# Attention scores of two heads issued in turn from two halves of the partitions, with masks and maxima regrouped, in a transformer block on one core

## The chip, the cores and the metric

The kernel runs on one core of one Trainium2 chip, in one launch. The metric is the device time of that launch in microseconds; lower is better. The core has five engines with a queue each: TensorE (PE, matmuls; PEld is its weight load), VectorE (DVE), ScalarE (ACT), GpSimd (POOL) and SyncE (SP, which here issues nearly all DMAs). They run side by side and wait for one another by semaphores.

## The reference, cut to what matters

One layer of a hybrid block on 512 tokens of width 1024: adaptive norm, a wide input projection, a gated linear attention (GLA) branch, a dilated attention branch, a merge, and a convolutional feed-forward part. The change is in the dilated attention. It has 3 groups of 4 heads of width 64; group 0 has dilation 1, group 1 dilation 4, group 2 dilation 16 (within 512 tokens the last two are both computed as 4 residues of 128 tokens, the last with a mask that keeps every fourth distance).

```python
q = rotary(aq...); k = rotary(ak...)
for g, (window, dilation) in enumerate(ATTN_GROUPS):       # per group, per head
    s = einsum('brhnid,brhnjd->brhnij', qb, kc) * (Dh ** -0.5)   # Dh = 64
    s = where(valid, s, -inf)
    m = max(s, axis=-1); p = exp(s - m); denom = sum(p)
    o = einsum('brhnij,brhnjd->brhnid', p, vc) / denom
    lse = m + log(denom)
o = sum(softmax(lse over groups) * o_g)
```

Everything is float32. The big projections are computed as three products of a high and a low part of each operand; the attention scores are plain float32 matmuls with a contraction of 64.

## The kernel before, in words

**Order of the work.** Each engine has one program, written out by hand. A list of weight units (256 columns of a weight matrix each) sets the order: value weights, six `qk` units (pair p of heads, group g), the low-rank unit `lr`, then per GLA head h the units `gqk`, `gv`, `gr`, and so on. For a unit ACT writes the high part (`split_hi`, L673), DVE the low part (`split_lo`, L1228), and TensorE multiplies in `product`, two tiles of 24 x 128x512 matmuls (L1773 to L1775, `three`). A tile takes one of two accumulator banks, so tile i+2 waits until the evacuation of tile i has freed its bank. The pieces of other work are put between the tiles: `attention(p, i)`, i from 0 to 6, exists on PE, DVE and ACT. For pair p=0 its parts stand between the tiles of the `qk` units of pair 1, `lr` and `gqk`; for p=1 between those of GLA head 0 and the first of head 1.

**A pair of heads.** The weights of unit (p, g) give q and k of both heads of the pair. DVE rotates them (`rotate`, L1298, L1299, L1302) into `rope`, SP copies them with eight DMAs (`shuffle`, L501) to `qk`, where a head's 64 dimensions stand on partitions 0 to 63, and the two heads beside each other along the free dimension. Parts 0 and 1 of `attention` on PE are `scores(hh)` for heads hh = 2p and 2p+1. A head has four score banks: bk 0 and 1 of group 0 (3 blocks of 256 columns and one of 128), bk 2 of group 1 and bk 3 of group 2 (4 blocks of 128 each). One fp32 matmul of the program is two weight loads and two matmuls in the trace. For p=0, part 0 does the first three banks of head 0, and part 1 the rest of head 0 and all of head 1. The banks are `side[bk]`, one for each bk, and the second head of a pair waits for the masks of the first.

**Masks and maxima.** On DVE `mask_and_max(hh)` adds a mask while it moves a bank to `S` in SBUF (L1323) and then takes row maxima (L1331 to L1337, L1342). When both heads are done, SP writes the maxima to DRAM and reads them back in the other order of tokens (`exchange(p)`, L533 and L538), DVE makes `negm` (part 3: L1355, L1359), ACT takes the exponentials (`exps`, parts 3 and 4, L798), PE transposes `S` (parts 4 and 5, L1928) and multiplies with the values (parts 5 and 6, L1947 to L1955). On SP's queue `shuffle(3)` stands ahead of `exchange(0)`; it overwrites `qk` and therefore waits until all scores of pair 0 are done (`sc_done` 8). ACT's evacuation of the tiles of `gqk` of head 0 (L928) waits for all scores of pair 1, since `q_in` lies where `qk` lay.

In DVE's order, after unit `qk` (1,1) has been split, part 1 stands ahead of the rotation of that unit's first tile.

Of the kernel before, what the change touches and what calls it, by code (L numbers as in the profile page):

```python
# [7 lines left out]
F32 = mybir.dt.float32  # L8
# [4 lines left out]
ALU = mybir.AluOpType  # L13
# [3 lines left out]
P = 128  # L17
SEQ = 512
D = 1024
KT = D // P  # L20
NB = SEQ // P
# [6 lines left out]
DH = 64  # L28
# [143 lines left out]
def hybrid_block_kernel(nc, x, c, positions, ada_w, ada_b, norm1_w, w_in, gate_w2, gate_b, gla_norm_w,  # L172
# [3 lines left out]
    with ctx:  # L176
# [29 lines left out]
        def region(*places):  # L206
# [26 lines left out]
        qk, rope, oa_hi, oa_lo, ocomb, osum, orec, oa32, rope_t, v_ext, S, PT, mx, mx_other, mg, negm = region(  # L233
            ("qk", 0, [DH, GROUPS, 2, 2, SEQ], F32), ("rope", 24, [P, 2, 2, SEQ], F32),
            ("oa_hi", 32, [P, 2, SEQ], F32R), ("oa_lo", 36, [P, 2, SEQ], F32R),
# [3 lines left out]
            ("PT", 95, [P, 1920], F32), ("mx", 102.5, [P, 8, 2], F32), ("mx_other", 102.625, [P, 8, 2], F32),  # L239
            ("mg", 102.75, [P, 2, 4], F32), ("negm", 107, [P, 8, 2], F32))  # L240

# [169 lines left out]
        BANK_W = [512, 384, 512, 512]  # L411

        def score_blocks(bk):

            if bk == 0:
                return [(0, 2 * P, 1), (2 * P, 2 * P, 2)]
            if bk == 1:
                return [(0, 2 * P, 3), (2 * P, P, 0)]
            return [(r * P, P, NB + r) for r in range(DIL)]
# [11 lines left out]
        def _(sp):  # L431
# [61 lines left out]
            def shuffle(j):  # L493

                p, g = divmod(j, GROUPS)
                sp.wait_ge(rope_sum, j + 1)
                if j == GROUPS:
                    sp.wait_ge(sc_done, 8)
                for half in range(2):
                    for a in range(4):  # L500
                        sp.dma_start(qk[32 * half:32 * half + 32, g, a // 2, a % 2, :],  # L501
                                     rope[32 * a:32 * a + 32, j % 2, half, :]).then_inc(qk_in[j % 2], 16)
# [633 lines left out]
        def _(dve):  # L1136
# [166 lines left out]

            def mask_and_max(hh, banks=range(4)):

                p, hd = divmod(hh, 2)
# [4 lines left out]
                for bk in banks:  # L1311
                    dve.wait_ge(sc_done, 4 * hh + bk + 1)
                    if hh >= 2:
                        dve.wait_ge(tr_ps, 4 * (hh - 2) + bk + 1)
                    at, w = BANK_AT[bk], BANK_W[bk]
                    dst, src = S[:, hd, at:at + w], side[bk][:, 0:w]
# [7 lines left out]
                for bk in banks:  # L1324
                    dve.wait_ge(msk_done, 4 * hh + bk + 1)
                    at = BANK_AT[bk]
                    if hd == 0 and bk == 0 and p > 0:
# [5 lines left out]
                    elif bk == 1:  # L1333
                        dve.tensor_reduce(mx[:, 3:4, hd], S[:, hd, at:at + 2 * P], AX.X, ALU.max)
                        dve.tensor_reduce(mx[:, 0:1, hd], S[:, hd, at + 2 * P:at + 3 * P], AX.X, ALU.max)
                    else:
                        dve.tensor_reduce(mg[:, bk - 2, :], S[:, hd, at:at + 4 * P].rearrange("p (a n) -> p a n", a=DIL),  # L1337
                                          AX.X, ALU.max).then_inc(mx1_done, 1)
                if 3 not in banks:
                    return  # L1340
                dve.wait_ge(mx1_done, 2 * hh + 2)
                dve.tensor_tensor(mx[:, NB:2 * NB, hd], mg[:, 0, :], mg[:, 1, :], ALU.max).then_inc(mx_done, 1)  # L1342
                dve.wait_ge(mx_done, hh + 1)

            def attention(p, i):

                if (p, i) == (0, 0):
                    mask_and_max(0, range(3))
                elif i in (0, 1):
                    if (p, i) == (0, 1):  # L1350
                        mask_and_max(0, range(3, 4))
                    mask_and_max(2 * p + i)
                if i == 3:
# [201 lines left out]
            for p in range(2):  # L1555
                for g in range(GROUPS):
# [8 lines left out]
                    elif g == 1:  # L1565
                        split_lo(n + 1)
                        attention(0, 1)
                        rotate(GROUPS + g, 0)
                        attention(0, 2)
# [197 lines left out]
        def _(pe):  # L1767
# [125 lines left out]

            def scores(hh, banks=range(4)):
                p, hd = divmod(hh, 2)
                if hh == 0:
                    pe.wait_ge(vw_act, NB)
                    pe.wait_ge(vw_dve, NB)
                for bk in banks:
                    if hh >= 1:  # L1900
                        pe.wait_ge(msk_done, 4 * (hh - 1) + bk + 1)
                    if hd == 0:
                        j = GROUPS * p + max(bk - 1, 0)
                        pe.wait_ge(qk_in[j % 2], 16 * 8 * (j // 2 + 1))
                    if hd == 0 and p > 0:
                        pe.wait_ge(pt_act if bk < 2 else pt_dve, 4 * p)
                    if bk < 2:
                        blocks = [(0, 1), (2 * P, 2)] if bk == 0 else [(0, 3), (2 * P, 0)]
                        for col, b in blocks:
                            lo = max(b - 1, 0) * P  # L1910
                            keys = slice(lo, (b + 1) * P)
                            last = pe.matmul(side[bk][:, col:col + (b + 1) * P - lo], qk[:, 0, 0, hd, b * P:(b + 1) * P],  # L1912
                                             qk[:, 0, 1, hd, keys], start=True, stop=True, skip_group_check=True)
                    else:
                        for r in range(DIL):
                            tok = slice(r * P, (r + 1) * P)
                            last = pe.matmul(side[bk][:, r * P:(r + 1) * P], qk[:, bk - 1, 0, hd, tok],  # L1917
                                             qk[:, bk - 1, 1, hd, tok], start=True, stop=True, skip_group_check=True)
                    last.then_inc(sc_done, 1)

# [38 lines left out]
            def attention(p, i):  # L1959

                if (p, i) == (0, 0):
                    scores(0, range(3))
                elif (p, i) == (0, 1):
                    scores(0, range(3, 4))
                    scores(1)
                elif i in (0, 1):
                    scores(2 * p + i)
                if i == 4:
# [400 lines left out]
```

## Time and profile before

| | us |
|---|---|
| median of 3 runs | 918.63 (918.57 to 919.01) |
| the profiled execution, its own time | 917.4 |
| its span in the trace | 915.6 |
| TensorE busy | 898.0 (98%) |
| VectorE busy | 494.4 (54%) |
| ScalarE busy | 368.7 (40%) |

The profiled execution is one run, 1.2 us below the median of the others. Its time is 1.8 us longer than the span of instructions in the trace. Busy time of TensorE includes overlap of matmuls in the pipeline, so the mean duration of a matmul is longer than the distance from one to the next. The granted TensorE clock was 0.997 over the whole execution.

### The profile page before, as it was taken

The numbers are of one execution on the slowest core, as the hardware profiler recorded it, in microseconds if no ns is written. First come the engines' busy times: TensorE is split into PE (matmuls) and PEld (weight loads), VectorE is DVE, ScalarE is ACT, GpSimd is POOL, SyncE is SP. The second block draws the span as 40 slices with busy tenths as digits, with TensorE's granted clock in tenths as the row PEclk, the third lists the DMA queues.
The fourth block names the chain that finished last, engine by engine and source line by source line (L and its number), as shares of the span: only waits on it lengthen the run. The fifth ranks groups of instructions, "written<-read, shape, count | busy, mean of one in ns | idle before, by whom it ended". The sixth has DMA issues, their size and how long they took to land.

```text
span 915.6 us, 11818 instructions
## 1 busy us (share of the span) xinstructions
PE 898.0 (98%) x4635; PEld 767.8 (84%) x4635; DVE 494.4 (54%) x580; ACT 368.7 (40%) x461; POOL 35.9 (4%) x33
## 2 busy tenths in 40 slices
PE   6999999999999999999999999999999999999996
PEld 6998888889898988888888888888888888888885
DVE  6878875636462646542544476555555556422223
ACT  6541226593534365332223345333333334322235
POOL 0010000000000000000021210000000000000003
PEclk9999999999999999999999999999999999999998
DMA  9976745115251525452233431333333332332202
GB/s 326 301 240 165 191 98 157 48 47 184 92 185 47 184 93 184 144 179 92 80 119 133 129 93 47 92 94 105 107 106 92 92 92 92 121 109 92 92 0 92
DMA packets 117133, 112.91 MB, mean 123 GB/s; under 512 B 7412, under 2 KB 107126, under 8 KB 114663
## 3 DMA queue, kind: packets, MB, share of 16 engines
q1 hardware_dynamic: 116375, 110.21, 38.6%
q10 hardware_dynamic: 720, 2.16, 0.7%
q8 instruction: 27, 0.44, 0.2%
q14 instruction: 11, 0.09, 0.0%
HBM read 104.80 MB, written 4.21 MB: 119 GB/s over the span
## 4 chain that ended last, share of the span: by engine, by line
PE 92%; DVE 3%; SPq 2%; DMA 1%; issue 1%; ACT 0%; DVEq 0%; ACTq 0%
PE bank L1773 27%; PE bank L1774 26%; PE bank L1775 26%; DVE ada_in L1155 1%; PE bank L2280 1%; DMA ada_in<-in_ada_w_dram 1%; SPq L446 1%; PE bank L1917 1%; PE bank L1955 1%; PE bank L2045 1%; PE bank L2013 1%; PE bank L1912 1%; PE bank L1928 1%; PE bank L1889 1%; SPq L510 1%
## 5 line engine op out<-in xcount | busy, mean ns | idle before, releaser
L1773 PE MATMUL bank<-h_hi,w_hi 128*128 128x512 f32 x672 | 264.7, 394 | 0.0
L1775 PE MATMUL bank<-h_hi,w_lo 128*128 128x512 f32 x672 | 261.7, 389 | 0.0
L1774 PE MATMUL bank<-h_lo,w_hi 128*128 128x512 f32 x672 | 261.6, 389 | 0.0
L1775 PEld LDWEIGHTS bank<-h_hi,w_lo 128*128 128x128 f32 x672 | 126.1, 188 | 26.6
L1773 PEld LDWEIGHTS bank<-h_hi,w_hi 128*128 128x128 f32 x672 | 126.2, 188 | 25.9 <-issue 0.2
L1774 PEld LDWEIGHTS bank<-h_lo,w_hi 128*128 128x128 f32 x672 | 126.2, 188 | 25.4 <-issue 0.2
L1228 DVE TENSOR_TENSOR w_lo<-raw,w_hi 128x2048 fp32r<-128x2048 f32 (+2 forms) x44 | 81.0, 1854 | 86.9 <-ACT w_hi L673 86.9
L1235 DVE TENSOR_TENSOR w_lo<-raw,w_hi 128x2048 fp32r<-128x2048 f32 x31 | 71.1, 2293 | 86.3 <-ACT w_hi L681 86.3
L1727 DVE SCALAR_TENSOR_TENSOR conv<-bank,vecs,conv 128x511 f32<-128x511 f32 x88 | 65.7, 748 | 65.8 <-ACT conv L1087 60.3
L681 ACT ACTIVATE w_hi<-raw 128x2048 fp32r<-128x2048 f32 x31 | 59.1, 1906 | 69.3 <-PE bank L1775 69.3
L673 ACT ACTIVATE w_hi<-raw 128x2048 fp32r<-128x2048 f32 (+2 forms) x42 | 67.9, 1630 | 46.9 <-DMA raw<-in_w_in_dram 34.2
L1087 ACT ACTIVATE conv<-bank,vecs 128x512 f32<-128x512 f32 x44 | 34.2, 779 | 104.7 <-PE bank L1775 104.7
L1773 PE MATMUL bank<-hs_hi,w_hi 128*128 128x512 f32 x176 | 68.6, 389 | 0.0
L1775 PE MATMUL bank<-hs_hi,w_lo 128*128 128x512 f32 x176 | 68.5, 389 | 0.0
L1774 PE MATMUL bank<-hs_lo,w_hi 128*128 128x512 f32 x176 | 68.5, 389 | 0.0
L1775 PEld LDWEIGHTS bank<-hs_hi,w_lo 128*128 128x128 f32 x176 | 33.0, 188 | 6.9
L1774 PEld LDWEIGHTS bank<-hs_lo,w_hi 128*128 128x128 f32 x176 | 33.0, 188 | 6.8
L1773 PEld LDWEIGHTS bank<-hs_hi,w_hi 128*128 128x128 f32 x176 | 33.0, 188 | 6.8
L1773 PE MATMUL bank<-w_hi,h_hi 128*128 128x256 f32 x128 | 36.5, 285 | 0.1
L1775 PE MATMUL bank<-w_hi,h_lo 128*128 128x256 f32 x128 | 36.2, 283 | 0.0
L1774 PE MATMUL bank<-w_lo,h_hi 128*128 128x256 f32 x128 | 36.2, 283 | 0.0
L1262 DVE SCALAR_TENSOR_TENSOR ada_acc<-raw,c_silu,ada_acc 128x2048 f32<-128x2048 f32 x14 | 32.9, 2346 | 0.0
(282 smaller groups left out, 1253.7 us busy)
## 6 DMA issues: line engine op xcount, KB each, us to landing
raw<-in_w_up_dram SPq DMA_DIRECT2D x44, 512.0 KB, 5.0
raw<-in_w_in_dram SPq DMA_DIRECT2D x17, 1024.0 KB, 5.3
raw<-in_ada_w_dram SPq DMA_DIRECT2D x16, 1024.0 KB, 5.5
raw<-in_w_in_dram SPq DMA_DIRECT2D x22, 512.0 KB, 5.3
raw<-in_w_down_dram SPq DMA_DIRECT2D x22, 512.0 KB, 3.7
ada_in<-in_ada_w_dram SPq DMA_DIRECT2D x16, 512.0 KB, 9.5
raw<-in_w_gla_branch_dram SPq DMA_DIRECT2D x4, 1024.0 KB, 4.9
raw<-in_w_out_dram SPq DMA_DIRECT2D x4, 1024.0 KB, 5.0
```

What stands on the lines that cost most here:

```text
L446: sp.dma_start(ada_first(j, half)[:, :, s_, :], ada_t[:, rows, s_, 2 * j * P:2 * (j + 1) * P]).then_inc(ada_landed[2 * j + half], 16)
L510: sp.dma_start(dst[:, rows, :], w_in_v[:, rows, at:at + width]).then_inc(first_in[n] if part == 0 else landed[n], 16)
L673: last = act.activation(hv, r, ACT.Copy)
L681: act.activation(w_hi[:, slot, :], raw[:, slot, :], ACT.Copy).then_inc(hi_done, 1)
L1087: act.activation(conv[:, s, t, :], bank[2 * (1 - s) + t][:, :], ACT.Identity, scale=vecs[:, bass.ds(i + (V_CW2 + t * FT), 1)], bias=vecs[: ...
L1228: last = dve.tensor_tensor(lv, r, hv.bitcast(F32), ALU.subtract)
L1235: dve.tensor_tensor(w_lo[:, slot, :], raw[:, slot, :], w_hi[:, slot, :].bitcast(F32), ALU.subtract).then_inc(raw_used, 1)
L1262: ins = dve.scalar_tensor_tensor(ada_acc[:, :], src, c_silu[:, k:k + 1], ada_acc[:, :], ALU.mult, ALU.add)
L1727: ins = dve.scalar_tensor_tensor(conv[:, s, t, tap:SEQ], src[:, 0:SEQ - tap], vecs[:, bass.ds(i + (col + t * FT), 1)], conv[:, s, t, tap:S ...
L1773: pe.matmul(out_ap, wh, xh, start=first, stop=False, skip_group_check=True)
L1774: pe.matmul(out_ap, wh, xl, start=False, stop=False, skip_group_check=True)
L1775: return pe.matmul(out_ap, wl, xh, start=False, stop=last, skip_group_check=True)
```

## The change

It has four parts.

1. `qk` becomes `[P, GROUPS, 2, SEQ]`: head 0 of the pair on partitions 0 to 63, head 1 on partitions 64 to 127. The eight DMAs of `shuffle` keep their number and size and change their targets.
2. `scores(p, bk)` issues each block for head 0 and then the same block for head 1, from the two halves of the partitions. The banks are `side[bk % 2 * 2 + hd]`. Part 0 does bk 0 and 1 of both heads, part 1 bk 2 and 3 of both. bk 2 and 3 wait for the masks of bk 0 and 1; for p=1 all four banks wait for the copies of pair 0 at the start.
3. On DVE `mask_and_max` becomes `masks(p, bk)` and `maxima(p, bk)`, each for both heads. A part does its four masks ahead of its four (or six) maxima. The two last combinations stand together at the end of part 1.
4. In the unit (1,1), DVE rotates the unit's first tile ahead of part 1 of pair 0.

```diff
-            ("qk", 0, [DH, GROUPS, 2, 2, SEQ], F32), ("rope", 24, [P, 2, 2, SEQ], F32),
+            ("qk", 0, [P, GROUPS, 2, SEQ], F32), ("rope", 24, [P, 2, 2, SEQ], F32),
...
-            ("mg", 102.75, [P, 2, 4], F32), ("negm", 107, [P, 8, 2], F32))
+            ("mg", 102.75, [P, 2, 2, 4], F32), ("negm", 107, [P, 8, 2], F32))
...
+        def score_bank(bk, hd):
+            return side[bk % 2 * 2 + hd]
...
-                        sp.dma_start(qk[32 * half:32 * half + 32, g, a // 2, a % 2, :],
+                        at = a % 2 * DH + 32 * half
+                        sp.dma_start(qk[at:at + 32, g, a // 2, :],
                                      rope[32 * a:32 * a + 32, j % 2, half, :]).then_inc(qk_in[j % 2], 16)
...
+            def masks(p, bk):
...
+                for hd in range(2):
+                    dve.wait_ge(sc_done, 8 * p + 2 * bk + hd + 1)
+                    if p > 0:
+                        dve.wait_ge(tr_ps, 8 * (p - 1) + 4 * hd + bk + 1)
+                    dst, src = S[:, hd, at:at + w], score_bank(bk, hd)[:, 0:w]
...
             def attention(p, i):
-                if (p, i) == (0, 0):
-                    mask_and_max(0, range(3))
-                elif i in (0, 1):
-                    if (p, i) == (0, 1):
-                        mask_and_max(0, range(3, 4))
-                    mask_and_max(2 * p + i)
+                if i in (0, 1):
+                    for bk in (2 * i, 2 * i + 1):
+                        masks(p, bk)
+                    for bk in (2 * i, 2 * i + 1):
+                        maxima(p, bk)
...
                     elif g == 1:
                         split_lo(n + 1)
+                        rotate(GROUPS + g, 0)
                         attention(0, 1)
-                        rotate(GROUPS + g, 0)
                         attention(0, 2)
                         rotate(GROUPS + g, 1)
...
+            def scores(p, bk):
+                if p == 0 and bk == 0:
+                    pe.wait_ge(vw_act, NB)
+                    pe.wait_ge(vw_dve, NB)
+                if p > 0 and bk == 0:
+                    pe.wait_ge(pt_act, 4 * p)
+                    pe.wait_ge(pt_dve, 4 * p)
+                if bk >= 2:
+                    pe.wait_ge(msk_done, 8 * p + 2 * (bk - 2) + 2)
...
+                for n, (col, queries, keys) in enumerate(parts):
+                    for hd in range(2):
+                        rows = slice(hd * DH, (hd + 1) * DH)
+                        last = pe.matmul(score_bank(bk, hd)[:, col:col + keys.stop - keys.start], qk[rows, g, 0, queries],
+                                         qk[rows, g, 1, keys], start=True, stop=True, skip_group_check=True)
+                        if n == len(parts) - 1:
+                            last.then_inc(sc_done, 1)
```

On TensorE, part 0 of pair 0 between two product tiles is, in the kernel before (L1773 to L1775 are the tiles, L1912 is group 0, L1917 groups 1 and 2; `x3` counts matmuls in a row, and both heads use partitions 0 to 63):

```order
L1775 MATMUL bank<-h_hi,w_lo 128x512
L1912 MATMUL bank<-qk 128x256 x3
L1912 MATMUL bank<-qk 128x128
L1917 MATMUL bank<-qk 128x128 x4
L1773 MATMUL bank<-h_hi,w_hi 128x512
```

and now (L1780 to L1782 are the tiles, L1923 all scores):

```order
L1782 MATMUL bank<-h_hi,w_lo 128x512
L1923 MATMUL bank<-qk 128x256 x6
L1923 MATMUL bank<-qk 128x128 x2
L1780 MATMUL bank<-h_hi,w_hi 128x512
L1781 MATMUL bank<-h_lo,w_hi 128x512
```

Part 0 keeps eight matmuls; they are now all of group 0, and neighbours belong to different heads. Part 1 of pair 0, one tile later on TensorE, was:

```order
L1775 MATMUL bank<-h_hi,w_lo 128x512
L1917 MATMUL bank<-qk 128x128 x4
L1912 MATMUL bank<-qk 128x256 x3
L1912 MATMUL bank<-qk 128x128
L1917 MATMUL bank<-qk 128x128 x8
L1773 MATMUL bank<-h_hi,w_hi 128x512
```

and is now:

```order
L1782 MATMUL bank<-h_hi,w_lo 128x512
L1923 MATMUL bank<-qk 128x128 x16
L1780 MATMUL bank<-h_hi,w_hi 128x512
L1781 MATMUL bank<-h_lo,w_hi 128x512
L1782 MATMUL bank<-h_hi,w_lo 128x512
```

It keeps sixteen matmuls too, now all of 128 columns and of groups 1 and 2.

On VectorE, from the split of unit (1,2) (the weights `w_lo`) to the end of part 1, the kernel before has:

```order
L1228 TENSOR_TENSOR w_lo<-raw,w_hi 128x8x128 x2
L1323 TENSOR_TENSOR S<-bank,cst 128x512
L1337 TENSOR_REDUCE mg<-S 128x4
L1342 TENSOR_TENSOR mx<-mg 128x4
L1323 TENSOR_TENSOR S<-bank,cst 128x512
L1323 TENSOR_TENSOR S<-bank,cst 128x384
L1323 TENSOR_TENSOR S<-bank,cst 128x512 x2
L1331 TENSOR_REDUCE mx<-S 128x2
L1334 TENSOR_REDUCE mx<-S 128x1
L1335 TENSOR_REDUCE mx<-S 128x1
L1337 TENSOR_REDUCE mg<-S 128x4 x2
L1342 TENSOR_TENSOR mx<-mg 128x4
```

and now:

```order
L1233 TENSOR_TENSOR w_lo<-raw,w_hi 128x8x128 x2
L1303 TENSOR_TENSOR rope<-bank,cs 128x512
L1304 SCALAR_TENSOR_TENSOR rope_t<-bank,cs 128x512
L1327 TENSOR_TENSOR S<-bank,cst 128x512 x4
L1344 TENSOR_REDUCE mg<-S 128x4 x4
L1350 TENSOR_TENSOR mx<-mg 128x4 x2
```

The rotation of one tile (`rope`, `rope_t`) has moved ahead of the masks, and the masks and maxima of group 0 of the second head have moved to part 0, ahead of this piece.

## Rows read from the trace of the kernel before

**Rows 1.** The page: busy time and share of TensorE; then the chain's shares.

```profile
PE 898.0 (98%) x4635; PEld 767.8 (84%) x4635; DVE 494.4 (54%) x580; ACT 368.7 (40%) x461; POOL 35.9 (4%) x33
...
PE 92%; DVE 3%; SPq 2%; DMA 1%; issue 1%; ACT 0%; DVEq 0%; ACTq 0%
```

**Rows 2.** Groups on TensorE by shape: rows*weight columns, moving shape, count | busy us, mean ns.

```profile
L1917 PE MATMUL bank<-qk 64*128 64x128 f32 x64 | 8.1, 274 | 0.0
L1889 PE MATMUL bank<-ones,ada_acc 128*128 128x1 f32 x64 | 7.7, 237 | 0.0
L1912 PE MATMUL bank<-qk 64*128 64x256 f32 x24 | 6.1, 389 | 0.0
L2017 PE MATMUL bank<-q,enb 128*32 128x32 f32 x32 | 1.8, 199 | 0.0
```

**Rows 3.** The chain in order of time, score stretches: start us, us, what.

```profile
106.39 1.71 PE bank L1912 x8
108.10 0.89 PE bank L1917 x8
...
114.65 1.08 PE bank L1917 x8
115.74 1.52 PE bank L1912 x8
117.26 1.79 PE bank L1917 x16
...
154.88 1.71 PE bank L1912 x8
156.59 1.79 PE bank L1917 x16
...
167.64 0.61 ACT q_in L928
```

**Rows 4.** Timeline of DVE, parts 0 and 1 of pair 0: start us, us.

```profile
109.51 1.75 DVE L1323 TENSOR_TENSOR S<-bank,cst 128x512 f32<-128x512 f32 x3
111.17 0.68 DVE L1331 TENSOR_REDUCE mx<-S 128x2 f32<-128x512 f32 x1
...
112.29 0.68 DVE L1337 TENSOR_REDUCE mg<-S 128x4 f32<-128x512 f32 x1
112.88 2.35 DVE L1228 TENSOR_TENSOR w_lo<-raw,w_hi 128x1024 fp32r<-128x1024 f32 x2
...
117.42 2.35 DVE L1323 TENSOR_TENSOR S<-bank,cst 128x512 f32<-128x512 f32 x4
...
120.80 1.27 DVE L1337 TENSOR_REDUCE mg<-S 128x4 f32<-128x512 f32 x2
...
122.30 1.05 DVE L1298 TENSOR_TENSOR rope<-bank,cs 128x512 f32<-128x512 f32 x1
```

**Rows 5.** Timeline of SP's DMA issues, the maxima of pair 0.

```profile
119.14 5.66 SPq L501 DMA_DIRECT2D qk<-rope  x8
124.84 1.15 SPq L533 DMA_DIRECT2D mx_dram<-mx  x2
129.34 0.91 SPq L538 DMA_DIRECT2D mx_other<-mx_dram  x2
```

**Rows 6.** Timeline of ACT: exponentials of the first head of pairs 0 and 1.

```profile
132.69 3.95 ACT L798 ACTIVATE S<-S,negm 128x256 f32<-128x256 f32 x12 [7.36 <-DVE negm L1359]
...
181.40 3.94 ACT L798 ACTIVATE S<-S,negm 128x256 f32<-128x256 f32 x12
```

**Rows 7.** The chain in order of time, at the transposes of pair 0.

```profile
135.64 1.71 PE bank L1928 x15
```

**Rows 8.** Timeline of DVE, pair 1: masks, last combination, the maxima's return.

```profile
160.34 2.35 DVE L1323 TENSOR_TENSOR S<-bank,cst 128x512 f32<-128x512 f32 x4
...
170.60 0.17 DVE L1342 TENSOR_TENSOR mx<-mg 128x4 f32<-128x4 f32 x1
...
177.36 0.17 DVE L1355 TENSOR_TENSOR mx_other<-mx_other,mx 128x16 f32<-128x16 f32 x1 [2.49 <-DMA mx_other<-mx_dram]
```

More of the change, by code:

```diff
@@ L1302, in rotate @@
                     dve.tensor_tensor(rope[:, j % 2, :, :], rope[:, j % 2, :, :], rope_t[:, :, :], ALU.add).then_inc(rope_sum, 1)
-            def mask_and_max(hh, banks=range(4)):
-                p, hd = divmod(hh, 2)
+            def masks(p, bk):
                 prev_own, own = cst[:, C_MSK:C_MSK + 2 * P], cst[:, C_MSK + P:C_MSK + 2 * P]
@@ L1310, in mask_and_max @@
                 two = prev_own.rearrange("p (a n) -> p a n", a=1).broadcast_to((P, 2, 2 * P))
[L1311 to L1316, printed above, removed]
+                at, w = BANK_AT[bk], BANK_W[bk]
+                for hd in range(2):
[3 more added lines that the diff above has]
+                    dst, src = S[:, hd, at:at + w], score_bank(bk, hd)[:, 0:w]
                     if bk == 1:
@@ L1323, in mask_and_max, with maxima @@
                     dve.tensor_tensor(dst, src, m, ALU.add).then_inc(msk_done, 1)
-                for bk in banks:
-                    dve.wait_ge(msk_done, 4 * hh + bk + 1)
-                    at = BANK_AT[bk]
+            def maxima(p, bk):
+                at = BANK_AT[bk]
+                for hd in range(2):
+                    dve.wait_ge(msk_done, 8 * p + 2 * bk + hd + 1)
                     if hd == 0 and bk == 0 and p > 0:
@@ L1336, in mask_and_max @@
                     else:
-                        dve.tensor_reduce(mg[:, bk - 2, :], S[:, hd, at:at + 4 * P].rearrange("p (a n) -> p a n", a=DIL),
+                        dve.tensor_reduce(mg[:, hd, bk - 2, :], S[:, hd, at:at + 4 * P].rearrange("p (a n) -> p a n", a=DIL),
                                           AX.X, ALU.max).then_inc(mx1_done, 1)
-                if 3 not in banks:
+                if bk < 3:
                     return
-                dve.wait_ge(mx1_done, 2 * hh + 2)
-                dve.tensor_tensor(mx[:, NB:2 * NB, hd], mg[:, 0, :], mg[:, 1, :], ALU.max).then_inc(mx_done, 1)
-                dve.wait_ge(mx_done, hh + 1)
+                dve.wait_ge(mx1_done, 4 * (p + 1))
+                for hd in range(2):
+                    dve.tensor_tensor(mx[:, NB:2 * NB, hd], mg[:, hd, 0, :], mg[:, hd, 1, :], ALU.max).then_inc(mx_done, 1)
+                dve.wait_ge(mx_done, 2 * p + 2)
             def attention(p, i):
-                if (p, i) == (0, 0):
-                    mask_and_max(0, range(3))
-                elif i in (0, 1):
-                    if (p, i) == (0, 1):
-                        mask_and_max(0, range(3, 4))
-                    mask_and_max(2 * p + i)
+                if i in (0, 1):
[3 more added lines that the diff above has]
+                        maxima(p, bk)
                 if i == 3:
@@ L1892, in ada_part @@
                         last.then_inc(acc_ready, 1)
-            def scores(hh, banks=range(4)):
-                p, hd = divmod(hh, 2)
-                if hh == 0:
+            def scores(p, bk):
+                if p == 0 and bk == 0:
                     pe.wait_ge(vw_act, NB)
                     pe.wait_ge(vw_dve, NB)
[L1899 to L1919, printed above, removed]
@@ new lines, in scores @@
+                if p > 0 and bk == 0:
[3 more added lines that the diff above has]
+                    pe.wait_ge(msk_done, 8 * p + 2 * (bk - 2) + 2)
+                j = GROUPS * p + max(bk - 1, 0)
+                pe.wait_ge(qk_in[j % 2], 16 * 8 * (j // 2 + 1))
+                g = max(bk - 1, 0)
+                if bk < 2:
+                    parts = []
+                    for col, b in ([(0, 1), (2 * P, 2)] if bk == 0 else [(0, 3), (2 * P, 0)]):
+                        parts.append((col, slice(b * P, (b + 1) * P), slice(max(b - 1, 0) * P, (b + 1) * P)))
+                else:
+                    parts = [(r * P, slice(r * P, (r + 1) * P), slice(r * P, (r + 1) * P)) for r in range(DIL)]
@@ new lines, in scores @@
+                for n, (col, queries, keys) in enumerate(parts):
+                    for hd in range(2):
+                        rows = slice(hd * DH, (hd + 1) * DH)
[3 more added lines that the diff above has]
+                            last.then_inc(sc_done, 1)
@@ L1959, in attention @@
             def attention(p, i):
[L1961 to L1967, printed above, removed]
+                if i in (0, 1):
+                    for bk in (2 * i, 2 * i + 1):
+                        scores(p, bk)
                 if i == 4:
```

## The prediction

> **What bounds the kernel now.** I read the page first. TensorE is busy for 98% of the span, and 92% of the chain that ended last is TensorE [rows 1]. So only what shortens or stalls TensorE's own queue counts; DVE, ACT and SP matter where TensorE would wait for them. Next I read the chain in order of time where the scores stand [rows 3]. The reader is to see that score matmuls lie on the chain without a gap. Part 0 of pair 0 takes 1.71 + 0.89 = 2.60 us and part 1 takes 1.08 + 1.52 + 1.79 = 4.39 us, together 6.99 us. For pair 1 a part is a whole head, 1.71 + 1.79 = 3.50 us, and the second head repeats it (two such stretches): 7.00 us. All scores are 14.0 us in 96 trace matmuls. Third, the groups by shape [rows 2], to see how fast such matmuls follow one another, and last the timelines of DVE, SP and ACT [rows 4 to 6, 8], to see what comes due once TensorE is earlier.
>
> **Part by part: the scores on TensorE.** Nothing is removed: 24 blocks of 256 columns and 72 of 128 in the trace before and after. What can change is the distance between them. In the last stretch of groups 1 and 2 sixteen matmuls of 128 columns take 1.79 us, 0.112 us each [rows 3], though one lasts 274 ns [rows 2]. In the stretch at 115.74 six of 256 and two of 128 columns take 1.52 us; with 0.112 for the small ones that leaves 0.216 us for a large one. All of them use partitions 0 to 63, half the rows of the array. After the change neighbours use different halves. The trace has no two matmuls on different halves in a row, so this price is bounded from both sides:
> - Best: the halves work side by side. A program matmul is two trace matmuls on one half, A1 A2 B1 B2. A2 must follow A1, B1 can run beside A2, B2 beside the next A1. Each step of 0.112 (or 0.216) us then carries two. Part 0 (12 x 0.216 + 4 x 0.112 = 3.04 us in series) takes half, 1.52, plus 0.1 for the step that is half empty; part 1 (32 x 0.112 = 3.58) takes 1.79 + 0.06. That is 3.5 us for a pair in place of 7.0, a gain of 3.5 us for each pair.
> - Middle: every matmul is stepped by its weight load. The nearest rows are matmuls with one moving column: 64 of them are busy 7.7 us, 0.12 us each, as long as with 128 columns, so there the load of 128 weight columns sets the step; with 32 weight columns it is 1.8 / 32 = 0.056 us [rows 2]. The last row also says that a load and a matmul can be issued in 0.056 us, so issue alone doesn't forbid the best case. If loads of both halves share one path, a pair takes 48 x 0.112 = 5.4 us, a gain of 1.6.
> - Worst: no overlap, and each change of half waits for the matmul before to leave the array, 274 - 112 = 0.16 us. With 48 changes over the kernel that is a loss of 7.7 us.
>
> I take the best end. The 64-row operands leave the other half idle, the two heads write different PSUM banks (`side[0]` and `side[1]`, then `side[2]` and `side[3]`), and neither the issue rate nor the data forbids it. The Trainium skill, "TensorEngine Tiling (Array Packing)", Key Properties, says that different tiles can load weights and multiply in parallel; no run here shows it yet, and by it the sum is that of the best end. The Trainium skill, "TensorE: Matmul & The Clock Gate", LDWEIGHTS, says that a weight load goes by its columns and not by its rows. The trace agrees (0.12 against 0.056 us for 128 and 32 columns), and if this held for the pair as a whole, the sum would be that of the middle.
>
> **Pair 0 gives part of it back.** The transposes of pair 0 start at 135.64 on the chain, and 11 x 0.112 us later, at 136.9, comes the fourth bank [rows 7]. The exponentials of that bank end at 132.69 + 3.95 = 136.64 [rows 6]. So they are only 0.2 us ahead, and they must become earlier too. Their chain after the change, in the best case:
> - Masks of part 0 start at 109.51 as now (DVE is behind a rotation). Four masks last 2.3 us [rows 4], two times the maxima of group 0 at 112.29 - 111.17 = 1.1 each make 2.2, so part 0 ends at 114.0, not 112.9. The split takes 2.3 (116.3), the rotation that has moved ahead 2 x 1.0 (118.3), four masks 2.4 (120.7), four maxima 4 x 0.6 = 2.4 and the combinations 0.3: the maxima are ready at 123.4. Now they are ready at 122.3, where the rotation starts.
> - On SP `shuffle(3)` starts when the scores end. It would start at 115.8 in place of 119.14 and be through in 5.7 us, at 121.5. The writes of the maxima then wait for DVE until 123.4, in place of 124.84: 1.4 us earlier. The reads come 4.5 us behind the writes [rows 5], at 127.9. For pair 1 the whole way from the last combination to the use of the returned maxima is 177.36 - 170.60 = 6.8 us [rows 8]; the same from 123.4 gives 130.2. `negm` follows at 130.6. DVE is free by then: the tile that it rotates ahead of it would be rotated by about 129.
> - So the exponentials start at 130.6 in place of 132.69, 2.1 us earlier, and with the 0.2 of slack TensorE can be 2.3 us earlier at the transposes, of 3.5.
>
> The gain of pair 0 is thus 2.2 us (rounded down), and a new wait of about 1.2 us stands in the transposes. Behind it on TensorE are `lr`, the values and all later tiles, and ACT's copies and exponentials shift with it, so that none of them is late again.
>
> **The moved rotation** costs nothing by itself, as the same two instructions of 1.05 us. It has a use: in the kernel before they end at 122.30 + 2.0 = 124.3 [rows 4], just as TensorE wants that accumulator: its tile starts behind the scores at 119.05 and takes 114.65 - 108.99 = 5.66 us, to 124.7 [rows 3]. With TensorE 3.3 us earlier they would be late by that much if they had stayed; moved, they end at 118.3 and the tile begins at about 121.
>
> **Pair 1.** TensorE arrives 2.2 us earlier and gains 3.5 in parts 0 and 1. The masks, at 160.34 in the trace, follow the same shift to 158.1 and take 2.3 us; bk 2 needs the second mask at 159.3 and TensorE comes there at about 160, bk 3 needs the fourth at 160.4 and TensorE comes at 160.9. No wait. The last combination, 170.60 now [rows 8], comes after 158.1 + 2.3 + 2.2 + 2.4 + 2.7 = 167.7, so 2.9 us earlier; with the same exchange `negm` is there 0.4 us behind 177.36 - 2.9, at 174.9. The exponentials stand at 181.40 [rows 6] behind other work of ACT and move by 5.7 to 175.7. Slack 0.8 us, no new wait. ACT's L928 waits for all scores of pair 1 and starts at 167.64 and TensorE goes on behind its 0.61 us [rows 3]; this wait of 0.6 us stays, since scores are still last before it.
>
> **The rest.** The DMAs of `shuffle` keep number and size; their landing hides behind a tile of 5.4 us. The waits of part 0 for group 1's `qk` go away and cost nothing before. The semaphore for the copies of pair 0 is long set. Loads of weights are issued when a slot is freed, so they shift with the work; I cost them at nothing, and if one were late it would show on ACT's splits.
>
> **Sum.** 2.2 + 3.5 = 5.7 us off the profiled execution: 917.4 - 5.7 = 911.7. The median of the runs stands 1.2 above it, so 912.9; I say 913.0.
>
> **Rivals.**
> 1. Weight loads set the step (the middle bound). For: one column costs as much as 128. Against: those rows are on the same rows of the array, where a load and its forerunner can't be apart. The gain is 2 x 1.6 = 3.2 us, all kept, since pair 0 needs less than 2.3: 915.4. If a load is only started once the matmul before it has begun, just the distance between halves shrinks for the large blocks, 24 / 2 x 0.104 = 1.3 us: 917.3. I price the case at 916.
> 2. The halves do not overlap, the change does not do what it says: TensorE takes 14.0 us as before. DVE's last maxima of pair 1 come about 1 us later, which the slack of ACT hides. 918.6, within 0.3.
> 3. The other side: each change between halves drains the array. Place: the 48 changes in four stretches. Price: 0.16 us each, 7.7 us, 926.3. It would be slower by the margin from 1.84 / 48 = 0.04 us for a change, without overlap. For: 274 against 112 ns show how much of a matmul's life is in flight. Against: nothing in the trace changes tiles, and the entry from full tiles to 64 rows costs about 0.1 us.
> 4. The best case, but pair 0 keeps nothing, for instance because the writes of the maxima take as long as they like: 918.6 - 3.5 = 915.1. It belongs to the range of the forecast.
>
> **Numbers.** Forecast (halves overlap, 912.2 to 915) 0.57; loads set the step 0.21; no overlap 0.12; drain 0.10. A measurement of this kernel can tell 0.2%, 1.84 us, from no change. Faster: 0.57 and three quarters of 0.21, 0.73 less a little for what I don't see, 0.71. Same: 0.18. Slower: 0.11. The range for 8 in 10 reaches from 911.9 (nothing lost in pair 0 up to 1 us) to 918.6, which takes in the loads and half of the no-overlap case. Its likeliest part is 912.2 to 915.0.
>
> **What would show it.** Right: in the chain the scores of a pair take about 3.5 us, in two stretches of 1.6 and 1.85; neighbours start much less than 0.1 us apart; the rotation is ahead of the masks; the exponentials of pair 0 start near 130.6, and TensorE waits about 1.2 us for them in the transposes; those of pair 1 aren't waited for. Wrong: distances of 0.112 us for 128 columns (loads), or 0.27 (drain); exponentials later than 132, or a transposes stretch with no wait although TensorE is 3 us ahead; a wait for DVE's mask at bk 2 or 3 of pair 1.

## The result and the profile after

| | before | after |
|---|---|---|
| median of 6 runs each | 918.42 us | 912.43 us (912.18 to 912.98) |
| ratio, 95% interval | | 0.9936 [0.9923, 0.9949] |
| profiled execution, its span | 917.4, 915.6 | 912.18, 910.4 |
| TensorE busy | 898.0 | 891.1 |

The change makes the kernel faster by 6.0 us at the median; the interval is 4.7 to 7.1 us. The two profiled executions differ by 5.2 us. A second set of runs of the changed kernel gave 0.9946 [0.9934, 0.9958]. The forecast was 913.0. Part of the spread lies outside the span of instructions: the median span is 910.65 us in both sets of the changed kernel, while the medians of the time are 912.43 and 913.22, since the time outside the span is 1.8 us in some runs and 2.5 to 2.8 in others. Where small differences matter below, spans are compared too.

First the page of the changed kernel, part 1, and by shape the groups of score matmuls (columns as in [rows 2]):

```profile
PE 891.1 (98%) x4635; PEld 760.7 (84%) x4635; DVE 493.5 (54%) x580; ACT 368.7 (40%) x461; POOL 35.9 (4%) x33
```

```profile
L1923 PE MATMUL bank<-qk 64*128 64x128 f32 x72 | 4.9, 277 | 0.0
L1923 PE MATMUL bank<-qk 64*128 64x256 f32 x24 | 3.1, 393 | 0.0
```

The 96 matmuls are the same as in [rows 2], and one still lasts 277 or 393 ns. But together they are busy for 4.9 + 3.1 = 8.0 us, where [rows 2] have 8.1 + 6.1 = 14.2 us for 88 of the 96. They last as long as before and follow one another twice as fast. The other 4539 matmuls are unchanged, and the busy time of TensorE falls by 6.9 us. The span falls by 5.2, less than that: something of the gain is given back.

The timeline of TensorE (start us, us, what, then what ended the idle time before it) shows where the difference stands:

```profile
106.58 1.79 PE L1923 MATMUL bank<-qk 64*128 64x256 f32 x16
...
108.30 0.50 PE L1780 MATMUL bank<-h_hi,w_hi 128*128 128x512 f32 x1
...
113.96 2.06 PE L1923 MATMUL bank<-qk 64*128 64x128 f32 x32
...
115.95 0.50 PE L1780 MATMUL bank<-h_hi,w_hi 128*128 128x512 f32 x1
...
132.41 0.93 PE L1935 MATMUL bank<-cst,S 128*128 128x128 f32 x7
133.58 0.66 PE L1935 MATMUL bank<-cst,S 128*128 128x128 f32 x4 [0.25 <-ACT S L803]
134.75 0.66 PE L1935 MATMUL bank<-cst,S 128*128 128x128 f32 x4 [0.51 <-ACT S L803]
...
152.84 1.79 PE L1923 MATMUL bank<-qk 64*128 64x256 f32 x16
...
160.23 2.06 PE L1923 MATMUL bank<-qk 64*128 64x128 f32 x32
162.21 0.73 PE L1989 MATMUL bank<-w2s,lrT 98*128 98x512 f32 x2
```

The scores of pair 0 take 1.72 us from their start to the next tile in part 0 and 1.99 us in part 1, 3.7 us in place of 6.99 [rows 3]. The transposes (L1935), one stretch without a gap in [rows 7], are now in three pieces and wait for ScalarE's exponentials before the third and the fourth bank. The scores of pair 1 take 1.72 + 2.04 us on the chain below, and their masks don't hold them up.

The trace also has the start of each single matmul. In part 1 of pair 0 the first two start at 113.961 and 113.968, 7 ns apart, and from the second pair on such a pair follows every 0.112 us. The last of each head in bank 2, known by the semaphore that it raises, are 6 ns apart (114.845 and 114.851). So the blocks A1 A2 of head 0 and B1 B2 of head 1 do not run as A1, A2 beside B1, B2 beside the next A1: B1 starts beside A1, ahead of A2. Only the way in and out of a stretch costs more than the usual step: 0.214 us from the first matmul to the next on its half, and 0.201 from the last to the tile, against 0.112. The kernel before has the same (0.213 into part 1, 0.202 out of part 0), so a stretch takes 0.19 us beyond its steps.

The chain of the changed kernel, in order of time, goes another way in pair 0 (start us, us, what):

```profile
120.62 2.38 DVE mg L1344 x4
...
123.30 0.37 SPq L538
...
123.71 4.16 DMA mx_dram<-mx
...
127.89 0.36 SPq L543
...
128.29 2.01 DMA mx_other<-mx_dram
...
130.75 3.96 ACT S L803 x12
...
134.75 0.66 PE bank L1935 x4
...
152.91 1.72 PE bank L1923 x16
...
160.30 2.04 PE bank L1923 x32
```

Before, the chain stayed on TensorE through this stretch. Now it runs through the last maxima on VectorE, the write of the maxima to DRAM, the read, and the exponentials, and comes back to TensorE at 134.75.

VectorE is the one that releases the write here, but only just. On SP's timeline the shuffle ends at 122.86, 0.4 us before the maxima are written out:

```profile
116.31 0.38 SPq L479 DMA_DIRECT2D raw<-in_w_in_dram  x1
116.74 0.58 SPq L480 DMA_DIRECT2D raw<-in_w_in_dram  x1
117.44 5.42 SPq L506 DMA_DIRECT2D qk<-rope  x8
```

The shuffle starts 1.5 us behind the end of the scores (115.95). Ahead of it on SP's queue stand two weight loads. They are issued 0.02 us after VectorE has ended a split (116.29), and that split starts 1.0 us later than in the kernel before, as part 0 now has two times the maxima of group 0. In the profiles of e2 and d1 below, SP writes the maxima directly behind the shuffle (123.67 and 124.72), though they are ready since 123.56 and 123.54.

The wait itself varies from one execution to the next. In the profile of the second set of the changed kernel TensorE waits once, and not twice:

```profile
132.87 1.53 PE L1935 MATMUL bank<-cst,S 128*128 128x128 f32 x11
134.91 0.66 PE L1935 MATMUL bank<-cst,S 128*128 128x128 f32 x4 [0.51 <-ACT S L803]
```

The account in profiled time: up to the end of the transposes the changed kernel is 137.35 - 135.40 = 1.95 us ahead, and since its scores happened to start 0.27 us later, pair 0 gave 2.2 us. From there to the end of the scores of pair 1 it takes 26.94 us (135.40 to 162.34) in place of 30.21 (137.35 to 167.56), 3.3 us less. Behind that the distance stays at 5.2 us to the end.

### The profile page after: what moved, and what is told of

Same layout as the page of the kernel before. It is cut to its first block, busy times and chain, and to the rows that moved or that the text cites. A ratio compares the mean times of both kernels' runs of the same rounds, so it can differ in the third digit from the quotient of the medians.

```text
span 910.4 us, 11817 instructions
## 1 busy us (share of the span) xinstructions
PE 891.1 (98%) x4635; PEld 760.7 (84%) x4635; DVE 493.5 (54%) x580; ACT 368.7 (40%) x461; POOL 35.9 (4%) x33
## 3 DMA queue, kind: packets, MB, share of 16 engines
q10 hardware_dynamic: 720, 2.16, 0.7%
## 4 chain that ended last, share of the span: by engine, by line
PE 87%; DVE 5%; DMA 3%; SPq 2%; issue 1%; ACT 1%; DVEq 0%; ACTq 0%
PE bank L1780 25%; PE bank L1782 25%; PE bank L1781 25%; DVE ada_in L1160 1%; PE bank L2283 1%; DMA ada_in<-in_ada_w_dram 1%; SPq L450 1%; PE bank L1962 1%; PE bank L2048 1%; PE bank L2016 1%; DMA raw<-in_w_in_dram 1%; PE bank L1896 1%; PE bank L1935 1%; SPq L515 1%; PE bank L1957 1%
## 5 line engine op out<-in xcount | busy, mean ns | idle before, releaser
L1780 PE MATMUL bank<-h_hi,w_hi 128*128 128x512 f32 x672 | 264.7, 394 | 0.0
L1782 PE MATMUL bank<-h_hi,w_lo 128*128 128x512 f32 x672 | 261.7, 389 | 0.0
L1782 PEld LDWEIGHTS bank<-h_hi,w_lo 128*128 128x128 f32 x672 | 126.1, 188 | 26.6
L1780 PEld LDWEIGHTS bank<-h_hi,w_hi 128*128 128x128 f32 x672 | 126.2, 188 | 25.8 <-issue 0.2
L1780 PE MATMUL bank<-hs_hi,w_hi 128*128 128x512 f32 x176 | 68.6, 389 | 0.0
L1782 PE MATMUL bank<-hs_hi,w_lo 128*128 128x512 f32 x176 | 68.5, 389 | 0.0
L1782 PEld LDWEIGHTS bank<-hs_hi,w_lo 128*128 128x128 f32 x176 | 33.0, 188 | 6.9
L1780 PEld LDWEIGHTS bank<-hs_hi,w_hi 128*128 128x128 f32 x176 | 33.0, 188 | 6.7
L1780 PE MATMUL bank<-w_hi,h_hi 128*128 128x256 f32 x128 | 36.5, 285 | 0.1
L1782 PE MATMUL bank<-w_hi,h_lo 128*128 128x256 f32 x128 | 36.2, 283 | 0.0
```

The source lines that it names most:

```text
L1780: pe.matmul(out_ap, wh, xh, start=first, stop=False, skip_group_check=True)
L1782: return pe.matmul(out_ap, wl, xh, start=False, stop=last, skip_group_check=True)
```

## The experiments

Times are medians, and ratios are to the kernel before on the same chip. The changed kernel is the base unless said otherwise.

**Both heads on one half (e1).** The operands lie as in the kernel before, and the targets of `shuffle` with them; everything else is as changed.

```diff
-            ("qk", 0, [P, GROUPS, 2, SEQ], F32)
+            ("qk", 0, [DH, GROUPS, 2, 2, SEQ], F32)
...
-                        last = pe.matmul(..., qk[rows, g, 0, queries], qk[rows, g, 1, keys], ...)
+                        last = pe.matmul(..., qk[:, g, 0, hd, queries], qk[:, g, 1, hd, keys], ...)
```

Expected: 

> The changed kernel with the scores' operands of both heads on partitions 0 to 63 again, in turn, with the new banks, masks, maxima and rotation. Theory (the halves of the array overlap): scores take 14.0 us on the chain again, 0.112 us for 128 columns, the wait in the transposes of pair 0 goes, and the time is 918.4, within 0.6. Rival (the gain comes from the regrouped masks and the moved rotation): 912.4 to 914.

Measured: 918.25 us, ratio 0.9995 [0.9985, 1.0004]. The timeline of TensorE, its scores:

```profile
106.56 3.30 PE L1921 MATMUL bank<-qk 64*128 64x256 f32 x16
...
115.45 3.83 PE L1921 MATMUL bank<-qk 64*128 64x128 f32 x32
```

The whole gain is gone, so it comes from the halves; the regrouping and the moved rotation give nothing by themselves. The banks are those of the changed kernel, so the banks are not what lets the matmuls overlap. One detail was wrong: a wait of 0.51 us in the transposes is still there. The exponentials start at 133.68, 1.0 us later than in [rows 6], behind a read of the maxima that took 2.79 us on the chain. The 0.2 us by which they are in time in the kernel before is less than what the exchange varies by.

**Head by head within a bank (e2).** The halves stay, the order changes.

```diff
-                for n, (col, queries, keys) in enumerate(parts):
-                    for hd in range(2):
+                for hd in range(2):
+                    for n, (col, queries, keys) in enumerate(parts):
```

Expected: 

> The changed kernel with the two halves kept, but within a bank all blocks of head 0 ahead of those of head 1. Theory (only neighbours on different halves overlap): overlap is left at the seams, 8 in a pair, about 0.11 us each, so scores take some 12 us and the time is 916.5 to 917.5. Rival (work is spread over the halves whatever its order, since later matmuls are pulled ahead): as the changed kernel, 912.4.

Measured: 914.34 us, ratio 0.9948 [0.9935, 0.9961]. Neither theory gave this number. The timeline of TensorE:

```profile
106.85 1.89 PE L1923 MATMUL bank<-qk 64*128 64x256 f32 x16
114.35 2.82 PE L1923 MATMUL bank<-qk 64*128 64x128 f32 x32
```

In part 0 four matmuls follow one another on a half, and it loses 0.1 us. In part 1 eight do, and it takes 2.82 us, between 2.06 (in turn) and 3.83 (one half). A strict order, in which only the last of a run shares its step with the first of the next, would make 13 steps in part 0, ten of 0.216 us and three of 0.112, 2.5 us, and 29 steps of 0.112, 3.2 us, in part 1, each without the 0.19 us in and out. So the two halves don't take their matmuls strictly in the order of the program.

The starts of the single matmuls show how they do it. In part 1 the eight of head 0 in bank 2 start from 114.354 to 115.237, and the first of head 1 at 114.908, 6 ns behind the fifth of head 0. Three of head 0 have still to start then. At the next two changes of half it is again the fifth (115.457 and 115.462, then 116.011 and 116.017). In part 0, with four in a run, head 1 starts 14 ns behind the first of head 0, again past three.

**Two blocks and two (e5).** To pin that down, runs of four on a half in both parts:

```diff
-                for n, (col, queries, keys) in enumerate(parts):
-                    for hd in range(2):
+                for n, hd, (col, queries, keys) in [(m + i, hd, parts[m + i]) for m in range(0, len(parts), 2)
+                                                    for hd in range(2) for i in range(2)]:
+                    for _ in range(1):
```

Expected: 

> The changed kernel with two blocks of head 0 and then two of head 1 in turn, so that four trace matmuls follow one another on a half. Theory from the run head by head, where only runs of eight lost time (matmuls on the other half start ahead of some four waiting ones): part 1 takes 2.0 us as with one and one, 912.4. Rival (strict order, one shared step for each run of four): 25 steps of 0.112 us, 2.8 us for part 1, 914.

Measured: 913.07 us, ratio 0.9939 [0.9926, 0.9952], beside 913.22 us, 0.9946, for the changed kernel on that chip. The timeline:

```profile
106.92 1.89 PE L1924 MATMUL bank<-qk 64*128 64x256 f32 x16
114.43 2.16 PE L1924 MATMUL bank<-qk 64*128 64x128 f32 x32
```

Part 1 takes 2.16 us, not 2.8. Runs of four trace matmuls cost 0.1 us for a stretch, runs of eight 0.76. The starts fit e2: in part 1 the first of head 1 starts 14 ns behind the first of head 0, with three of head 0 still to start. So in these two kernels a matmul goes past three waiting trace matmuls of the other half and not past four: in e2, when the fourth of head 0 starts at 114.791 with four behind it, nothing of head 1 starts. What sets this reach no run shows.

**Scores twice, in turn (d1) and on one half (d2, from the kernel before).**

```diff
+                parts = parts + parts
```

In the kernel before the lists of blocks and of residues are doubled in the same way. Each block is computed twice into the same place.

Expected for d1: 

> The changed kernel with every score block computed twice into the same place, in turn between the halves. Theory (halves overlap, a pair's scores cost 3.75 us): 7.5 us more, less the 1.2 us of waiting in the transposes of pair 0, so about 918.7. Rival (each matmul is stepped by its weight load, 0.112 us): 10.8 us more, 922 to 923.

Expected for d2: 

> The kernel before with every score block computed twice into the same place. Both theories: 14.0 us more, 932.4; this is the price of the scores on one half measured on the whole kernel. Less would mean that part of the scores was not on the path.

Measured: d1 918.06 us, ratio 0.9997 [0.9988, 1.0006], 5.6 us above the changed kernel; d2 931.09 us, ratio 1.0139 [1.0124, 1.0155], 12.8 us (11.4 to 14.2) above the kernel before. The timelines, first d1, then d2:

```profile
106.83 3.31 PE L1924 MATMUL bank<-qk 64*128 64x256 f32 x32
...
115.73 3.84 PE L1924 MATMUL bank<-qk 64*128 64x128 f32 x64
...
135.97 1.87 PE L1936 MATMUL bank<-cst,S 128*128 128x128 f32 x15
```

```profile
161.56 3.30 PE L1912 MATMUL bank<-qk 64*128 64x256 f32 x16
164.70 3.73 PE L1917 MATMUL bank<-qk 64*128 64x128 f32 x32
```

Twice the matmuls in turn cost what the single ones cost on one half. The second 32 of part 1 add 3.84 - 2.06 = 1.78 us, 0.056 us each: half of 0.112, with nothing lost. With 3.31 - 1.79 = 1.52 for part 0 that is 3.3 us more for a pair, 6.6 in all; the kernel loses only 5.6, because the transposes of pair 0 have no wait any more (x15 in one piece). This supports both terms, the price of a pair and the wait. d2 doubles the scores on one half: the fence shows one head of pair 1. The expected 14.0 us took the way in and out of each stretch twice; the added matmuls alone are 24 x 0.216 + 72 x 0.112 = 13.2 us, and the median spans differ by 929.3 - 916.3 = 13.0. If each matmul were stepped by its weight load, d1 had been 922 or more.

**The rotation back behind part 1 (e3, e3b).**

```diff
-                        rotate(GROUPS + g, 0)
                         attention(0, 1)
+                        rotate(GROUPS + g, 0)
```

Expected: 

> The changed kernel with the rotation behind the masks and maxima of part 1 again. The rotation would end at about 123.1, and TensorE wants the accumulator at 121.4: a wait of 1.7 us before the tile. Theory: the wait of 1.2 us in the transposes, behind it, shrinks by as much, and the time is 912.6 to 913.2. Rival (waits add up): 914.1.

Expected of the repeat: 

> The changed kernel with the rotation behind part 1 again, a second time and beside the changed kernel. Its first profile shows TensorE waiting 1.34 us for the rotation and no longer for the exponentials. Theory: 0.5 us above the changed kernel. Rival (the waits add up): 1.3 us or more above it.

Measured: 914.22 us (five runs, two near 913.0 and three near 914.3), ratio 0.9944 [0.9930, 0.9957]; in the repeat 912.95 us, 0.9948 [0.9935, 0.9961], where the changed kernel had 913.22 and 0.9946. The timeline of TensorE of the first:

```profile
123.48 0.50 PE L1780 MATMUL bank<-h_hi,w_hi 128*128 128x512 f32 x1 [1.34 <-DVE rope_t L1304]
...
134.54 1.86 PE L1935 MATMUL bank<-cst,S 128*128 128x128 f32 x15
```

The wait is where it was expected, 1.34 us for the rotation (1.7 expected), and the one in the transposes is gone. So most of one wait replaces the other, and they do not add up. By the time alone the first set would have looked like the rival. The median spans are 911.5 and 911.2 us, 0.85 and 0.55 above the 910.65 of the changed kernel. The profiles agree: from the start of the scores of pair 0 to the gate matmuls behind those of pair 1 (L1989) it takes 56.17 and 56.36 us, and 55.63 and 55.35 in the two profiles of the changed kernel. The move of the rotation is worth some 0.5 to 0.9 us here, less than its wait, as the exponentials hold TensorE anyway. In e3 the maxima are ready at 121.38, but SP writes them at 122.94, behind the shuffle: the earlier maxima don't bring the exchange forward by as much.

**The moved rotation alone, in the kernel before (e4).** The same two lines.

Expected: 

> The kernel before with the moved rotation alone. Theory: it frees an accumulator that TensorE does not wait for, so 918.4 within 0.4; the maxima come 2 us later, hidden since the exchange stands behind the shuffle. Rival (the moved rotation is part of the gain): under 917.5.

Measured: 918.99 us, ratio 1.0013 [0.9999, 1.0027]. No gain. In its profile SP issues the write of the maxima directly behind the shuffle (125.81), as in [rows 5], so the later maxima, ready at 124.63, don't hold anything. TensorE does wait in the transposes here, which in the profile of the kernel before it didn't:

```profile
138.17 0.66 PE L1928 MATMUL bank<-cst,S 128*128 128x128 f32 x4 [0.36 <-ACT S L798]
```

From write to read the exchange took 5.0 us and not 4.5; as in e1, being in time by 0.2 us is no more than chance. The scores started 1.0 us later than in the profile of the kernel before, which is a difference between two executions and not the change's.

**The exchange of group 0 early (f1).** The maxima of group 0 are ready at the end of part 0. They are written ahead of the shuffle and read back ahead of the wait for the others.

```diff
+                if part == 0:
+                    sp.wait_ge(mx0_done, 6)
+                    sp.dma_start(own[0], mx[:, 0:NB, :]).then_inc(mx_out, 16)
+                    return
+                if part == 1:
+                    sp.wait_ge(mx_out, 16)
+                    sp.dma_start(mx_other[:, NB:2 * NB, :], other[1]).then_inc(mx_in, 16)
+                    sp.wait_ge(mx_done, 2)
+                    sp.dma_start(own[1], mx[:, NB:2 * NB, :]).then_inc(mx_out, 16)
+                    sp.wait_ge(mx_out, 32)
+                    sp.dma_start(mx_other[:, 0:NB, :], other[0]).then_inc(mx_in, 16)
+                    return
```

Expected: 

> The changed kernel with the exchange of the maxima of pair 0 in two steps: the maxima of group 0 are written before the shuffle and read back before those of groups 1 and 2 are ready; these follow alone. Theory (the exponentials of pair 0 hold TensorE through the exchange): negm comes when DVE is free, at about 129.7 and not 130.5, the wait in the transposes goes, 1.0 us less, 911.4. Rival (the wait comes back elsewhere, or the remaining DMAs take as long as all four): 912.4.

Measured: 911.36 us, ratio 0.9925 [0.9911, 0.9939], 1.1 us below the changed kernel's median of 912.43. Its timeline of SP's issues, of DVE and of TensorE:

```profile
124.24 0.58 SPq L542 DMA_DIRECT2D mx_other<-mx_dram  x1
124.86 0.45 SPq L544 DMA_DIRECT2D mx_dram<-mx  x1
126.57 0.37 SPq L546 DMA_DIRECT2D mx_other<-mx_dram  x1
```

```profile
129.28 0.17 DVE L1376 TENSOR_TENSOR mx_other<-mx_other,mx 128x16 f32<-128x16 f32 x1
```

```profile
132.49 1.86 PE L1949 MATMUL bank<-cst,S 128*128 128x128 f32 x15
```

From the last write to the last read it is 1.7 us, not 4.6. The write in 8-byte pieces, which has gone ahead, took 3.3 us to land by itself; the one in 32-byte pieces that is left lands within 1.7. VectorE no longer waits for the maxima (130.33 in the changed kernel), and the transposes are one piece. The intervals of f1 and of the changed kernel overlap, but every span of f1 (909.3 to 910.3 us) is below every one of the changed kernel (910.4 and more), and the profile shows the wait taken out at its place. That the exchange was what held pair 0 is shown.

**The score operands apart (f2).** `qk` now needs 12 KB of a partition, not 24; at 8 KB it lies clear of `q_in` and `k_in`.

```diff
-            ("qk", 0, [P, GROUPS, 2, SEQ], F32)
+            ("qk", 8, [P, GROUPS, 2, SEQ], F32)
...
-                    if a < 2:
-                        act.wait_ge(sc_done, 16)
-                    else:
+                    if a >= 2:
```

Expected: 

> The changed kernel with the now smaller score operands placed apart from the GLA queries and keys, so that ScalarE's evacuation of these need not wait for the scores of pair 1. Theory: the evacuation leaves the chain, where it stands with 0.73 us between the last score and the next tile, of which a bit over 0.1 stays: 0.6 us less, 911.8. Rival: the next wait takes its place, 912.4.

Measured: 912.37 us, ratio 0.9933 [0.9920, 0.9947]: nothing beside 912.43. Its timeline of TensorE behind the last score:

```profile
162.94 0.73 PE L1987 MATMUL bank<-w2s,lrT 98*128 98x512 f32 x2
163.51 0.28 PE L1778 MATMUL bank<-w_hi,h_hi 128*128 128x256 f32 x1
```

In the changed kernel the gate matmuls L1989 start at 162.21 and the next tile at 163.07, here it is 162.94 and 163.51: 0.3 us less, not 0.6. About half of the 0.61 us that the chain gave to ScalarE was filled by TensorE's own gate matmuls. The time hides the 0.3, the spans hint at it: their median is 910.3 us, 0.35 below the changed kernel's. In the profiled execution the scores of pair 0 started 0.73 us later than in the changed kernel's profile (107.31), and L1987 is still 0.73 later; at the end of the span it is 0.4 (910.8 against 910.4), so 0.3 came in behind the scores of pair 1.

**Both (f3).**

Expected: 

> The changed kernel with the early exchange of group 0's maxima and the score operands placed apart, both together. The first gave 1.0 us; the second shortened the step from the gate matmuls to the next tile from 0.86 to 0.57 us, which its own time did not show. Theory: 1.3 us below the changed kernel, 911.1. Rival (the second is worth nothing): 911.4.

Measured: 911.01 us, ratio 0.9920 [0.9907, 0.9933], where the changed kernel had 913.22, 0.9946 [0.9934, 0.9958], on the same chip. It is the fastest kernel here, 2.2 us below the changed one in that set and 7.5 below the kernel before. The median span is 909.2 us, 1.45 below the changed kernel's; f1 alone was 1.05 below it (909.6) and f2 0.35 (910.3). So the two gains add up, and the placement is worth 0.3 to 0.4 us as far as these medians can tell.

The changed kernel itself was run beside it. Expected: 

> The changed kernel itself, to stand beside the others of this chip: 912.4, ratio 0.9935.

Measured: 913.22 us, a ratio of 0.9946 within the interval of its first set, and the same median span, 910.65 us.

## Why the prediction was right

- **The overlap of the halves** (best end, 3.5 us for a pair): right. Measured 3.3 and 3.3. Each stretch is 0.10 to 0.14 us longer than worked out, 1.72 and 1.99 against 1.62 and 1.85: the sum left out the way in and out, 0.19 us, though the prediction names some 0.1 us for the way in under its third rival, and counted a half empty step of 0.1 and 0.06 that isn't there. e1 shows that it is the halves, d1 that the step is 0.056 us for each matmul, or 0.112 for two on different halves. The bound from weight loads is out: each of these matmuls has its load of 128 columns, and in the changed kernel those of both halves start 7 ns apart, so the rows of one-column matmuls spoke of loads on the same rows. The Trainium skill, "TensorEngine Tiling (Array Packing)", Key Properties, says that different tiles load weights and multiply in parallel. These runs agree with it.
- **How they overlap**: wrong in the order, right in the sum. The model in the prediction has A1 with nothing and A2 beside B1; the trace has B1 beside A1. In turn the two orders differ by one step in a stretch. With longer runs they differ by much, and e2 and e5 show the looser one.
- **Pair 0 gives part back** (2.2 of 3.5): right, measured 2.2, and in part by luck, as the exchange varies by more than the error: the second profile of the changed kernel has only one of the two waits, and the scores-to-transposes time is 28.5 us in it and 28.8 in the first, against 31.0 before. Maxima ready at 123.3 (123.4 expected), reads at 127.89 (127.9), exponentials at 130.75 (130.6). The shuffle started at 117.44 and not at 115.8 and ended at 122.9 and not at 121.5; this stayed hidden by 0.4 us. The wait in the transposes is 0.25 + 0.51 us on TensorE's timeline, 1.2 us with the restarts of its weight loads: its fifteen matmuls and what lies between take from 132.41 to 135.40 in place of 1.8 us.
- **The moved rotation** as a cost of nothing and of use once TensorE is early: half right. Without it TensorE waits, but since the exponentials are waited for later, the kernel loses only part of it. The prediction gave it 3.3 us of lateness; measured are 1.34 and 1.55, since VectorE's masks come earlier too (116.26 in e3, 117.42 before), and by its own chain 1.2 of it would be paid at the transposes in any case. It was no term of the sum.
- **Pair 1** (3.5, no new wait): 3.3 measured. The last maxima came at 167.85 (167.7 expected), the exponentials at 176.16 (175.7).
- **ACT's evacuation as a wait of 0.6 us that stays**: it stays, but f2 shows that only about 0.3 us of it was waiting.
- **The sum**: 5.7 expected, 5.2 in the profiled executions and 6.0 between the medians. 5.5 without the later start at 106.58. That the time comes within 0.6 us of 913.0 is two errors that partly cancel: the profiled execution took 912.18 and not 911.7, and the median stands 0.25 us above it and not 1.2.

## What to carry to other kernels

Matmuls with a contraction of 64 that come in independent pairs can be put on two halves of the partitions, with results in different banks; alternating single ones is best, runs of four trace matmuls cost 0.1 us for a stretch, runs of eight lose some 0.4 of the gain. Where TensorE is the bound and gets faster by such a step, list what was only just in time for it before (here the exponentials, 0.2 us ahead), and follow each back to what isn't sped up: here an exchange through DRAM of which half could leave earlier. A releaser on the chain is not yet idle time; look whether the waiting engine had other work beside it.

## What the runs showed of the hardware

- fp32 matmuls with 64 rows and 128 columns follow one another after 0.112 us on one half and after 0.056 us in turn on both, weight loads of 128 columns included. With 256 columns it is 0.216 and 0.108.
- Four matmuls in a row on a half overlap with the other half's almost fully (2.16 against 2.06 us for 32), eight partly (2.82); a strict order would give 2.8 and 3.2. By the starts in e2 and e5 a matmul goes ahead of three waiting ones of the other half, and not of four.
- The step from a 128x512 tile into a stretch of 64-row matmuls and out of it costs 0.19 us beyond the usual steps, counted from the first start of the stretch to the tile's, on one half and on two alike (before and after).
- Alternating halves needs no drain: d1 has 96 matmuls of the program in four stretches with no more than the 0.056 or 0.108 us for each trace matmul.
- A write of 4 KB to DRAM in 8-byte pieces and one in larger pieces together took 4.2 us until the reads were issued; with the small-piece one sent ahead, the other took 1.7. By itself the one in 8-byte pieces landed after 3.3 us (f1). The reads of pair 0 took 1.9 to 2.8 us over the profiles, a spread of 0.9 us, more than the 0.2 us that the exponentials had to spare.
